# Expert numbers of quarters 1 to 7 of each pass, made from places by GpSimd instead of VectorE

## The chip, the cores and the metric

The kernel runs on one core of one Trainium2 chip. The metric is the device time of one execution in microseconds. Engines are named as the profile names them: PE is TensorE, DVE is VectorE, ACT is ScalarE, POOL is GpSimd, SP is the queue engine.

## The reference

Two layers of a transformer block over 256 latent tokens of width 1024 and 256 context tokens: three kinds of attention, a gated merge, and then an expert layer (PEER). What the change touches is how an expert is chosen:

```python
s = jnp.einsum('thpd,hpkd->thpk', q, keys)                 # 8 heads, two sides, 128 keys each
sv, si = lax.top_k(s, PEER_TOPK)                           # the 16 best keys of each side
cand_s = sv[:, :, 0, :, None] + sv[:, :, 1, None, :]       # 16 x 16 sums
cand_i = si[:, :, 0, :, None] * PEER_KEYS + si[:, :, 1, None, :]
top_s, pos = lax.top_k(cand_s, PEER_TOPK)                  # the 16 best sums and their places
e = jnp.take_along_axis(cand_i, pos, axis=-1)              # the expert numbers
g = jax.nn.softmax(top_s, axis=-1)
act = jax.nn.gelu(jnp.einsum('thkd,td->thk', u[e], tc))
return jnp.einsum('thk,thkd->td', g * act, v[e])
```

So each token picks 8 heads x 16 = 128 rows out of 16384, and of each row the part u is multiplied with the token and the part v is added up.

## The kernel before

**Passes.** The expert layer runs three times, in passes of 256 tokens: pass 0 (layer 0, latent tokens), pass 1 (layer 0, context tokens) and pass 2 (layer 1, latent tokens). A pass takes 256 *picks*. One pick is one gather: 128 partitions each fetch one expert row of 8 KB (u and v together), 1 MB, by an indirect DMA whose addresses are one column of `index`. An even pick serves 64 tokens, with two rows for each, and the odd one behind it the next 64. The 256 picks are divided into eight *quarters* of 32 (the name is the kernel's), each of which needs its own columns of `index` before its first gather.

**The loop over picks** stands on four engines, each in its own order:
- POOL (`gather`, L1848 to L1860) waits until the pair of picks that used the buffer eight picks ago is released (`row_used`), then issues the gather into one of eight buffers (L1854).
- DVE (`gather`, L2420 to L2432) waits for the rows (`rows_in`) and makes the dot of u with the token (L2426), 1024 elements.
- ACT makes the gelu, the weight and a scaled selection matrix of it (L1651, L1653, L1658).
- PE multiplies that matrix with v (L1252), four products for a pick, and releases a pair of buffers (`row_used`).

**What else runs there.** Between two dots DVE, ACT and PE each take steps of other work, called *ticks*: `PICKS_AT` says after which picks a tick of choosing experts stands, `TOKENS_AT` after which a tick of the rest (in pass 0 the whole attention and merge of the context tokens, in pass 1 the modulation and the projection of layer 1). Weight transfers for it come over SP's queue on the same sixteen DMA engines. The first quarter of a pass is chosen before its gathers, or for pass 1 at the end of pass 0.

**Choosing a quarter** (`picks_of`, DVE) takes seven ticks. Ticks 0 to 2 find the 16 best sums out of 112 candidates. Tick 3 turns their positions into *places*, for each pick a number 0 to 15 on either side (L2257 to L2269). Ticks 4 and 5 turn places into key numbers: for side w, compare the places with 0 to 15 (L2275, into `hot`, 128 x 512), multiply with the key numbers `sif` (L2276), add up over 16 (L2277, into `chosen`). Tick 5 then joins both sides to an expert number and writes `index` (L2280, L2283), tick 6 writes the softmax gates. `hot` lies in the same words as `work`, which the searches for the best use.

**Where the ticks stand.** Quarter 1 and quarter 2 of passes 0 and 2 have a tick every two picks, quarter 3 about every four, quarters 4 to 7 every four or five. In pass 1 all seven have one every two picks. Of quarter 2 of pass 2, for instance, tick 3 stands after the dot of pick 47 and tick 5 after that of pick 51; of its quarter 4 they stand after picks 97 and 107.

## Time and profile before

| | |
|---|---|
| median of 3 runs | 3107.65 us (3103.76 to 3109.70) |
| profiled execution | 3107.62 us, its span 3105.8 us |
| busy: PE, DVE, ACT, POOL | 2330.2 (75%), 1855.6 (60%), 1233.0 (40%), 849.2 (27%) us |
| mean granted PE clock | 0.866 |
| gathers (software queue): packets, MB, share of 16 DMA engines | 112032, 810.08, 63.8% |
| weights (hardware queue): packets, MB, share | 27216, 196.45, 16.4% |
| chain that ended last, by engine | PE 42%, DMA 30%, DVE 15%, ACT 6% |

The first gather of pass 0 starts 512.1 us into the span, that of pass 1 at 1321.5, that of pass 2 at 2426.8, and the last at 3071.1. The shares of busy time are averages over stages with different limits; what a change in the gather passes is worth has to be read there, from the share of the DMA engines in a window and from the times at which single gathers start and their dots start. A row's number in square brackets is idle time of its engine just before it, and behind the arrow what ended it.

### The profile page before, as it was taken

Reading aid. Unit: us, or ns where it says so; the run is one execution under the profiler, and the core shown is the slowest. Engines: PE = TensorE matmul, PEld = TensorE weight load, DVE = VectorE, ACT = ScalarE, POOL = GpSimd, SP = SyncE. Lnnn points to the kernel's source line nnn. Section 1 sums busy time; section 2 is a strip of 40 time slices with the busy share of each in tenths; the row PEclk is TensorE's granted clock in tenths of the full one; section 3 lists DMA queues with packets and bytes.
Section 4 is the critical chain, followed back from the end, with each engine's and each line's share of the span. In section 5 each row is a group of like instructions: output and inputs, shape, how many; then the busy total and the mean of one; then the engine's idle time right before and its main releaser. Section 6 shows DMA issues by size and latency. Waiting matters only on the chain.

```text
span 3105.8 us, 33307 instructions
## 1 busy us (share of the span) xinstructions
PE 2330.2 (75%) x11404; PEld 1352.9 (44%) x11404; DVE 1855.6 (60%) x4461; ACT 1233.0 (40%) x3361; POOL 849.2 (27%) x790
## 2 busy tenths in 40 slices
PE   5998998777669989665656688768998865555565
PEld 3787896443336645221212344217798621111111
DVE  3328655776855554586657554455864687666654
ACT  4215533344843243342333433244643434333333
POOL 0000001333332233343334443320000344444442
PEclk8999998988989999787767999969999988878777
DMA  6531246989989999999999999963044899999996
GB/s 255 217 133 48 96 162 244 413 347 378 394 345 389 402 421 407 383 401 421 388 421 405 414 421 421 421 288 122 22 163 150 332 383 422 421 421 421 419 422 288
DMA packets 139705, 1011.33 MB, mean 326 GB/s; under 512 B 15632, under 2 KB 15760, under 8 KB 17168
## 3 DMA queue, kind: packets, MB, share of 16 engines
q0 software_dynamic: 112032, 810.08, 63.8%
q1 hardware_dynamic: 27216, 196.45, 16.4%
q10 hardware_dynamic: 288, 2.69, 0.2%
q8 instruction: 90, 1.47, 0.2%
q14 instruction: 79, 0.65, 0.1%
HBM read 1008.10 MB, written 1.05 MB: 325 GB/s over the span
## 4 chain that ended last, share of the span: by engine, by line
PE 42%; DMA 30%; DVE 15%; ACT 6%; issue 3%; POOL 3%; ACTq 0%; POOLq 0%; DVEq 0%; SPq 0%
DMA att<-experts_in,att 28%; PE ps L1252 13%; DVE att L2426 5%; PE ps L612 4%; PE ps L1112 4%; PE ps L614 4%; PE ps L613 4%; POOL att L1854 3%; DMA ring<-stream_in 2%; PE ps L913 2%; DVE ring_lo L1900 2%; PE ps L1162 2%; ACT wt_hi L1356 2%; ACT att L1658 1%; PE ps L879 1%
## 5 line engine op out<-in xcount | busy, mean ns | idle before, releaser
L1252 PE MATMUL ps<-att 128*64 128x512 f32 x3072 | 977.8, 771 | 660.7 <-ACT att L1658 654.0
L1854 POOL DMA_INDIRECT att<-experts_in,att x768 | 838.9, 1092 | 1785.5 <-PE ps L1252 1202.0
L2426 DVE CUSTOM_DVE_ANT_0 att<-att 128x1024 f32<-128x1024 f32 x768 | 930.2, 1224 | 626.9 <-DMA att<-experts_in,att 615.4
L1252 PEld LDWEIGHTS ps<-att 128*64 128x64 f32 x3072 | 224.6, 163 | 1279.9 <-ACT att L1658 918.0
L1651 ACT ACTIVATE att<-att 128x1 f32<-128x1 f32 x768 | 154.4, 201 | 1050.2 <-DVE att L2426 1040.2
L1900 DVE TENSOR_TENSOR ring_lo<-ring,wt_hi 128x2048 fp32r<-128x2048 f32 x68 | 155.8, 2292 | 250.0 <-ACT wt_hi L1356 249.9
L1658 ACT ACTIVATE att<-const,att 128x64 f32<-128x64 f32 x768 | 267.1, 348 | 71.7 <-ACT att L1653 1.5
L1653 ACT ACTIVATE att<-att 128x1 f32<-128x1 f32 x768 | 226.1, 294 | 25.1
L1356 ACT ACTIVATE wt_hi<-ring 128x2048 fp32r<-128x2048 f32 x68 | 129.7, 1910 | 164.1 <-PE ps L614 86.8
L612 PE MATMUL ps<-h,wt_hi 128*128 128x256 f32 (+1 forms) x360 | 114.5, 318 | 19.7 <-DVE h L1914 11.0
L1844 POOL DMA_DIRECT2D att<-bias_in x16 | 8.9, 556 | 436.2 <-DVE stat L2093 413.1
L613 PE MATMUL ps<-h,wt_hi 128*128 128x256 f32 (+1 forms) x360 | 112.4, 312 | 0.0
L614 PE MATMUL ps<-h,ring_lo 128*128 128x256 f32 (+1 forms) x360 | 112.2, 312 | 0.0
L1175 PE MATMUL ps<-spare,ring 128*128 128x256 f32 x384 | 87.5, 383 | 0.0
L1112 PE MATMUL ps<-spare,ring 128*128 128x256 f32 x384 | 86.9, 379 | 0.0
L612 PEld LDWEIGHTS ps<-h,wt_hi 128*128 128x128 f32 x360 | 71.8, 199 | 29.8 <-DVE ring_lo L1900 14.3
L770 PE MATMUL ps<-att,ring 128*128 128x256 f32 x336 | 81.1, 396 | 0.0
L1175 PEld LDWEIGHTS ps<-spare,ring 128*128 128x128 f32 x384 | 71.5, 190 | 22.0 <-issue 13.0
L1112 PEld LDWEIGHTS ps<-spare,ring 128*128 128x128 f32 x384 | 72.9, 190 | 11.1 <-issue 1.3
L770 PEld LDWEIGHTS ps<-att,ring 128*128 128x128 f32 x336 | 64.3, 197 | 28.3 <-issue 19.9
L613 PEld LDWEIGHTS ps<-h,wt_hi 128*128 128x128 f32 x360 | 71.8, 199 | 2.7
L614 PEld LDWEIGHTS ps<-h,ring_lo 128*128 128x128 f32 x360 | 71.7, 199 | 2.9
(252 smaller groups left out, 3678.4 us busy)
## 6 DMA issues: line engine op xcount, KB each, us to landing
ring<-stream_in SPq DMA_DIRECT2D x183, 1024.0 KB
att<-experts_in,att POOLq DMA_INDIRECT x768
att<-bias_in POOLq DMA_DIRECT2D x16, 256.0 KB, 2.9
spare<-stream_in SPq DMA_DIRECT2D x3, 1024.0 KB, 7.0
x<-x_in ACTq DMA_DIRECT2D x1, 2048.0 KB, 8.2
out<-att SPq DMA_DIRECT2D x1, 1024.0 KB, 3.9
const<-const_in ACTq DMA_DIRECT2D x1, 576.0 KB, 4.3
att<-lambda_in SPq DMA_DIRECT2D x1, 256.0 KB, 11.4
```

Source lines behind the costliest of these rows:

```text
L612: mm(dst, a[0], b[0], start=start, stop=False)
L613: mm(dst, a[0], b[1], start=False, stop=False)
L614: return mm(dst, a[1], b[0], start=False, stop=stop)
L1112: last = mm(ps[:, 2 + item % 6, 0:N_CTX], raw_slot(p0, b), src, start=(c == 0), stop=(c == count - 1))
L1175: last = mm(ps[:, pq_bank(r, u), 0:N_LAT], raw_slot(p0, u * DC + c), h2_plain[:, c, :], start=(c == 0), stop=(c == DC - 1))
L1252: last = mm(ps[HALF * s:HALF * (s + 1), d, :], diag[:, (m + s) % DIAGS, :], rows[:, (m + s) % SLOTS, D + 512 * d:D + 512 * (d + 1)], start ...
L1356: nc.scalar.activation(wt_hi[:, d % 2, :], ring[:, DENSE[d] % RING, :], ACT.Copy)\
L1653: nc.scalar.activation(acts[:, n:n + 1], acts[:, n:n + 1], ACT.Copy, scale=gates[:, r % 2, n:n + 1])\
L1658: nc.scalar.activation(diag[:, m % DIAGS, :], fold, ACT.Copy, scale=acts[:, n:n + 1])\
L1854: nc.gpsimd.indirect_dma_start(out=rows[:, m % SLOTS, :], out_offset=None, in_=experts_in, in_offset=bass.IndirectOffsetOnAxis(ap=index[:, ...
L1900: v.tensor_tensor(ring_lo[:, DENSE[d] % RING, :], ring[:, DENSE[d] % RING, :], wt_hi[:, d % 2, :], ALU.subtract)\
L2426: v.tensor_tensor_reduce(out=u_row, in0=u_row, in1=dup[:, n // HK, n % 2, :], scale=1.0, scalar=0.0, op0=ALU.mult, op1=ALU.add, accum_out= ...
```

## The change

POOL makes `chosen` from the places for quarters 1 to 7 of each pass; quarter 0 stays on DVE. The table `chosen_before` says ahead of which gathers the two sides stand: side 0 nine gathers behind the pick of tick 3, side 1 two gathers later. For quarter 2 of pass 2 these are gathers 56 and 58, for quarter 4 gathers 106 and 108, for quarter 6 of pass 1 gathers 108 and 110. POOL subtracts, compares with zero, multiplies, and adds up by halving: seven instructions for a side, each waiting for the one before by a semaphore. DVE's tick 4 is empty, and tick 5 waits for both sides.

```diff
@@
+def chosen_before(r):
+    at = {}
+    tick = SIDE_TICKS if r != 1 else 1 + SIDE_TICKS
+    for q in range(1, QUARTERS):
+        slot = PICKS_AT[r][tick + PICK_PLACES] | 1
+        for w in range(2):
+            at[min(slot + SLOTS + 1, q * QUARTER - 2) + 2 * w] = q, w
+        tick += PICK_TICKS
+        if q == 1:
+            tick += len(CTX_SIDES) * SIDE_TICKS + (1 if r == 1 else 0)
+    return at
@@ gpsimd
+            def after_step(ins):
+                steps_done[0] += 1
+                ins.then_inc(pool_order, 1)
+                pool.wait_ge(pool_order, steps_done[0])
+
+            def chosen_of(r, q, w):
+                pair = [P, 2, TOPK, TOPK]
+                steps16 = iota[:, 0:TOPK].unsqueeze(1).unsqueeze(1).to_broadcast(pair)
+                pool.wait_ge(places_ready, (QUARTERS - 1) * r + q)
+                at = places[:, w * QUARTER:(w + 1) * QUARTER].rearrange("p (h k) -> p h k", h=2)
+                after_step(nc.gpsimd.tensor_tensor(hot, steps16, at.unsqueeze(3).to_broadcast(pair), ALU.subtract))
+                after_step(nc.gpsimd.tensor_scalar(hot, hot, 0.0, None, ALU.is_equal))
+                after_step(nc.gpsimd.tensor_tensor(hot, hot, sif[:, :, w, :].unsqueeze(2).to_broadcast(pair), ALU.mult))
+                for half in (8, 4, 2):
+                    after_step(nc.gpsimd.tensor_tensor(hot[:, :, :, 0:half], hot[:, :, :, 0:half],
+                                                       hot[:, :, :, half:2 * half], ALU.add))
+                nc.gpsimd.tensor_tensor(chosen[:, w, :].rearrange("p (h k) -> p h k", h=2).unsqueeze(3),
+                                        hot[:, :, :, 0:1], hot[:, :, :, 1:2], ALU.add).then_inc(chosen_ready, 1)
+                pool.wait_ge(chosen_ready, 2 * ((QUARTERS - 1) * r + q - 1) + w + 1)
+
             def gather(r):
+                before = chosen_before(r)
                 for n in range(PICKS):
                     m = r * PICKS + n
+                    if n in before:
+                        chosen_of(r, *before[n])
@@ picks_of on DVE
+                if q:
+                    v.tensor_tensor(places[:, QUARTER:2 * QUARTER], next2, low2, ALU.add).then_inc(places_ready, 1)
+                    yield
+                    yield
+                    dve.wait_ge(chosen_ready, 2 * ((QUARTERS - 1) * r + q))
+                else:
+                    link(v.tensor_tensor(places[:, QUARTER:2 * QUARTER], next2, low2, ALU.add))
+                    yield
+                    for w in range(2):
+                        chosen_at_first(w)      # the three instructions as before
+                        if w == 0:
+                            yield
```

POOL, pass 2 from its start, as before (`att` is the large tile in which buffers, index and scratch lie):

```order
L1844 DMA att<-bias_in 128x512
L1844 DMA att<-bias_in 128x512 [waits max_ready] x6
L1854 DMA att<-experts_in,att 128x2048 [waits row_used,index_ready]
L1854 DMA att<-experts_in,att 128x2048 [waits row_used] x31
L1854 DMA att<-experts_in,att 128x2048 [waits row_used,index_ready]
```

POOL, pass 2 around gathers 106 to 108, as changed:

```order
L1899 DMA att<-experts_in,att 128x2048 [waits row_used] x9
L1879 TENSOR_TENSOR att<-const,att 128x512 [waits places_ready]
L1880 TENSOR_SCALAR att<-att 128x512 [waits pool_order]
L1881 TENSOR_TENSOR att<-att 128x512 [waits pool_order]
L1883 TENSOR_TENSOR att<-att 128x32x8 [waits pool_order]
L1883 TENSOR_TENSOR att<-att 128x32x4 [waits pool_order]
L1883 TENSOR_TENSOR att<-att 128x32x2 [waits pool_order]
L1885 TENSOR_TENSOR att<-att 128x32 [waits pool_order]
L1899 DMA att<-experts_in,att 128x2048 [waits row_used,chosen_ready]
L1899 DMA att<-experts_in,att 128x2048 [waits row_used]
L1879 TENSOR_TENSOR att<-const,att 128x512 [waits places_ready]
```

Seven instructions now stand ahead of gather 106 and seven ahead of gather 108, where only gathers stood.

DVE, quarter 2 of pass 2, from tick 4 to the dot behind tick 5, as before (L2426 is the dot, `rows_in` the semaphore of its buffer):

```order
L2275 TENSOR_TENSOR att<-const,att 128x512
L2276 TENSOR_TENSOR att<-att 128x512 [waits dve_order]
L2277 TENSOR_REDUCE att<-att 128x32 [waits dve_order]
L2426 ISA att<-att 128x1024 [waits rows_in2,dve_order]
L2426 ISA att 128x1
L2426 ISA att<-att 128x1024 [waits rows_in3]
L2426 ISA att 128x1
L2275 TENSOR_TENSOR att<-const,att 128x512
L2276 TENSOR_TENSOR att<-att 128x512 [waits dve_order]
L2277 TENSOR_REDUCE att<-att 128x32 [waits dve_order]
L2280 SCALAR_TENSOR_TENSOR att<-att 128x32 [waits dve_order]
L2283 TENSOR_SCALAR att<-att 64x16 [waits dve_order]
```

DVE at the same place, as changed (L2480 is the dot, L2334 and L2337 are what L2280 and L2283 were):

```order
L2480 ISA att 128x1
L2480 ISA att<-att 128x1024 [waits rows_in2]
L2480 ISA att 128x1
L2480 ISA att<-att 128x1024 [waits rows_in3]
L2480 ISA att 128x1
L2334 SCALAR_TENSOR_TENSOR att<-att 128x32 [waits chosen_ready]
L2337 TENSOR_SCALAR att<-att 64x16 [waits dve_order]
L2337 TENSOR_SCALAR att<-att 64x16 x3
L2480 ISA att<-att 128x1024 [waits rows_in4]
```

The six instructions are gone, and the first instruction of the index waits for POOL, with the dot of pick 52 behind it.

## Rows read from the trace of the kernel before

**Rows 1.** The page, busy share of the DMA engines in 40 slices of 77.6 us:

```profile
DMA  6531246989989999999999999963044899999996
```

**Rows 2.** Windows: stretch, us, busy PE, PEld, DVE, ACT, POOL (count), PEclk, DMA share, GB/s:

```profile
600.00:660.00 60.00, 37.22 (x125) 14.59 (x126) 55.11 (x214) 25.84 (x79) 19.09 (x18) 0.76 0.86 338
740.00:880.00 140.00, 94.64 (x528) 44.42 (x528) 115.05 (x275) 105.35 (x289) 49.94 (x48) 0.87 0.92 361
...
1500.00:1520.00 20.00, 12.84 (x55) 4.06 (x56) 12.73 (x29) 11.29 (x35) 8.20 (x8) 0.76 0.76 292
...
2560.00:3060.00 500.00, 281.77 (x806) 62.98 (x802) 307.31 (x664) 185.86 (x617) 219.24 (x201) 0.78 1.01 421
```

**Rows 3.** Timeline, pass 1: gather 60 (POOL) and its dot (DVE); start, length, idle before:

```profile
1506.85 0.94 POOL L1854 DMA_INDIRECT att<-experts_in,att  x1 [10.89 <-PE ps L1252]
...
1512.67 1.23 DVE L2426 CUSTOM_DVE_ANT_0 att<-att 128x1024 f32<-128x1024 f32 x1 [1.96 <-DMA att<-experts_in,att]
```

**Rows 4.** Timeline, pass 2, quarter 4: gathers 105, 106, 108 and the dot of 107:

```profile
2693.03 1.26 POOL L1854 DMA_INDIRECT att<-experts_in,att  x1 [0.30 <-issue]
...
2698.31 0.94 POOL L1854 DMA_INDIRECT att<-experts_in,att  x1 [4.02 <-PE ps L1252]
...
2701.73 0.94 POOL L1854 DMA_INDIRECT att<-experts_in,att  x1 [1.23 <-PE ps L1252]
...
2712.14 1.23 DVE L2426 CUSTOM_DVE_ANT_0 att<-att 128x1024 f32<-128x1024 f32 x1 [1.25 <-DMA att<-experts_in,att]
```

**Rows 5.** Groups by form (count, busy us, mean ns, idle before), and all gathers (ns min/median/max):

```profile
L2276 DVE TENSOR_TENSOR att<-att 128x512 f32<-128x512 f32 x48 | 33.2, 692 | 1.7
L2275 DVE TENSOR_TENSOR att<-const,att 128x512 f32<-128x512 f32 x48 | 33.0, 688 | 0.2
L2277 DVE TENSOR_REDUCE att<-att 128x32 f32<-128x512 f32 x48 | 32.9, 686 | 1.6
...
L2181 DVE TENSOR_TENSOR att<-att 128x256 f32<-128x256 f32 x32 | 13.6, 425 | 1.1
...
L1854 POOL DMA_INDIRECT att<-experts_in,att x768: 932/937/1992, 512.1 to 3071.1; - x192
```

**Rows 6.** Timeline, pass 2, quarter 2: gathers 55, 60; dots 51, 53, 57; index:

```profile
2568.96 1.03 POOL L1854 DMA_INDIRECT att<-experts_in,att  x1 [0.30 <-issue]
...
2571.59 1.22 DVE L2426 CUSTOM_DVE_ANT_0 att<-att 128x1024 f32<-128x1024 f32 x1 [0.43 <-DMA att<-experts_in,att]
...
2575.13 0.72 DVE L2283 TENSOR_SCALAR att<-att 64x16 uint32<-64x16 f32 x4
...
2577.03 1.22 DVE L2426 CUSTOM_DVE_ANT_0 att<-att 128x1024 f32<-128x1024 f32 x1
...
2582.92 1.09 POOL L1854 DMA_INDIRECT att<-experts_in,att  x1 [3.76 <-PE ps L1252]
...
2587.04 1.22 DVE L2426 CUSTOM_DVE_ANT_0 att<-att 128x1024 f32<-128x1024 f32 x1 [1.24 <-DMA att<-experts_in,att]
```

**Rows 7.** Timeline, pass 1, quarter 6: gathers 104 and 107, dot of 107:

```profile
1649.75 0.94 POOL L1854 DMA_INDIRECT att<-experts_in,att  x1 [10.36 <-PE ps L1252]
...
1654.54 1.03 POOL L1854 DMA_INDIRECT att<-experts_in,att  x1 [0.30 <-issue]
...
1664.52 1.22 DVE L2426 CUSTOM_DVE_ANT_0 att<-att 128x1024 f32<-128x1024 f32 x1 [1.02 <-DMA att<-experts_in,att]
```

**Rows 8.** Timeline, DVE's search behind quarter 1, passes 0 and 2, waiting for PE:

```profile
597.07 0.90 DVE L2202 MAX8 att<-ps 128x8 f32<-128x128 f32 x4 [5.63 <-PE ps L998]
...
2504.53 0.89 DVE L2202 MAX8 att<-ps 128x8 f32<-128x128 f32 x4 [5.76 <-PE ps L998]
```

**Rows 9.** Timeline, pass 1: gather 80 and its dot:

```profile
1566.95 1.68 POOL L1854 DMA_INDIRECT att<-experts_in,att  x1 [7.56 <-PE ps L1252]
...
1584.11 1.23 DVE L2426 CUSTOM_DVE_ANT_0 att<-att 128x1024 f32<-128x1024 f32 x1 [1.84 <-DMA att<-experts_in,att]
```

More of the change, by code:

```diff
@@ L82 @@
             BIASED[STEP0[_l] + _n] = len(BIASED)
-PICK_TICKS, PICK_EXP = 7, 4
+PICK_TICKS, PICK_EXP, PICK_PLACES = 7, 4, 3
 SIDE_TICKS = 2
@@ L128 @@
              spread(1, (REST_UNIT_TICKS, 28)) + spread(HK + 4, (UPDATE_TICKS, 16))]
+def chosen_before(r):
[8 more added lines that the diff above has]
+            tick += len(CTX_SIDES) * SIDE_TICKS + (1 if r == 1 else 0)
+    assert tick == len(PICKS_AT[r])
+    return at
 def due(at, n):
@@ L405, in build @@
         mod_cols_copied = sem("mod_cols_copied")
+        places_ready = sem("places_ready")
+        chosen_ready = sem("chosen_ready")
+        pool_order = sem("pool_order")
         mod_ready = sem("mod_ready")
@@ L1845, in biases @@
                         .then_inc(bias_arrived[b % 2], 16)
+            steps_done = [0]
+            def after_step(ins):
[16 more added lines that the diff above has]
+                pool.wait_ge(chosen_ready, 2 * ((QUARTERS - 1) * r + q - 1) + w + 1)
             def gather(r):
+                before = chosen_before(r)
                 for n in range(PICKS):
                     m = r * PICKS + n
+                    if n in before:
+                        chosen_of(r, *before[n])
                     if n % QUARTER == 0:
@@ L2224, in sides_of, with chosen_at_first @@
                 yield
+            def chosen_at_first(w):
+                pair = [P, 2, TOPK, TOPK]
+                steps16 = iota[:, 0:TOPK].unsqueeze(1).unsqueeze(1).to_broadcast(pair)
+                at = places[:, w * QUARTER:(w + 1) * QUARTER].rearrange("p (h k) -> p h k", h=2)
+                link(v.tensor_tensor(hot, steps16, at.unsqueeze(3).to_broadcast(pair), ALU.is_equal))
+                link(v.tensor_tensor(hot, hot, sif[:, :, w, :].unsqueeze(2).to_broadcast(pair), ALU.mult))
+                link(v.tensor_reduce(chosen[:, w, :].rearrange("p (h k) -> p h k", h=2), hot, AX.X, ALU.add))
             def picks_of(r, l, q):
@@ L2235, in placed @@
                         .rearrange("p (k s) -> p s k", s=2)[:, s, :]
-                pair = [P, 2, TOPK, TOPK]
                 dve.wait_ge(sides_found, 8 * r + 4 * tt + g + 1)
@@ L2268, in picks_of @@
                 link(v.scalar_tensor_tensor(next2, by16, 4.0, next2, ALU.is_lt, ALU.mult))
-                link(v.tensor_tensor(places[:, QUARTER:2 * QUARTER], next2, low2, ALU.add))
-                yield
-                steps16 = iota[:, 0:TOPK].unsqueeze(1).unsqueeze(1).to_broadcast(pair)
-                for w in range(2):
-                    at = places[:, w * QUARTER:(w + 1) * QUARTER].rearrange("p (h k) -> p h k", h=2)
-                    link(v.tensor_tensor(hot, steps16, at.unsqueeze(3).to_broadcast(pair), ALU.is_equal))
-                    link(v.tensor_tensor(hot, hot, sif[:, :, w, :].unsqueeze(2).to_broadcast(pair), ALU.mult))
-                    link(v.tensor_reduce(chosen[:, w, :].rearrange("p (h k) -> p h k", h=2), hot, AX.X, ALU.add))
-                    if w == 0:
-                        yield
+                if q:
[10 more added lines that the diff above has]
+                            yield
                 link(v.scalar_tensor_tensor(partsf[:, 0:QUARTER], chosen[:, 0, :], float(KEYS), chosen[:, 1, :],
```

## The prediction

> **What bounds the kernel now.** Read the row of slices first [rows 1]: the sixteen DMA engines stand at eight or nine tenths from slice 8 to slice 26 and again from slice 32 to slice 39, which is where the three gather passes lie. Then the windows [rows 2]: over the last 500 us of pass 2 the DMA share is 1.01 at 421 GB/s while DVE is busy 307 us of 500 and POOL 219. One gather moves 1 MB, 2.49 us at that rate. DVE is nearly full only in short stretches (55 of 60 us at 600 to 660, 115 of 140 at 740 to 880), and there the DMA share falls to 0.86 and 0.92. So time is gained only where DMA runs dry for DVE's sake, and lost wherever a gather is issued too late. This is why the two questions are how much DVE relief falls into the dry stretches, and how late GpSimd gets.
>
> **How late may it be?** The shortest way from issue to use in the trace is 5.8 us: the gather at 1506.85 came after GpSimd had waited 10.89 us, DMA had run dry (share 0.76 in 1500 to 1520, [rows 2]), and its dot began at 1512.67 [rows 3]. In the saturated part of pass 2 the way is longer because others are queued ahead: gather 106 of the pass goes out at 2698.31 and gather 107's dot starts at 2712.14 [rows 4]. A gather costs nothing as long as its issue plus 5.8 us is not behind the landing of the one before plus 2.49.
>
> **What is removed.** Per quarter DVE loses six instructions, twice 0.69 + 0.69 + 0.69 = 2.07 us [rows 5], 4.1 us, in 21 of 24 quarters: 87 us of 1856. In the saturated stretches DVE's idle time grows by that and nothing else happens. Quarters 3 and 4 of pass 0 lie in 740 to 880, where DVE is short: at most 2 x 4.1 = 8 us. I take half, since what follows in that stretch is not DVE's alone (ACT is busy 105 of the 140 us, [rows 2]): **minus 4 us**.
>
> **What is added.** Two chains of seven GpSimd instructions per quarter, each waiting for the one before: subtract, compare and multiply on 512 elements, then additions on 256, 128, 64 and 32. The trace has no GpSimd arithmetic, so the chain's price D is bounded. From below: DVE's prices, three times 0.69 and four times the 0.42 of a 256-element addition [rows 5], 3.8 us. From above: seven times GpSimd's own step, 0.94 us plus the 0.30 us in front of it [rows 4, 5], 8.7 us. I take seven times 0.94, **D = 6.6 us**, since a GpSimd row is nearer to GpSimd than DVE's, and since the wait for its own semaphore must cost something over 3.8.
>
> The Trainium skill (GPSIMD Engine Reference, section 3.1) measures a two-input addition at 1.96 times DVE's time. By that page alone the chain would be an estimated 6 to 7 us, and the sum nearly the one below.
>
> **Where the chains stand.** Chain 0 comes ahead of the gather nine behind the pick at which DVE writes the places, chain 1 two gathers on. Queued behind each are the gathers. DVE no longer computes; two ticks behind the places it waits for both chains, and behind that wait stand its dots, without which ACT and TensorE release no row. Where ticks are two picks apart (quarters 1 and 2 of passes 0 and 2, all of pass 1: the *tight* ones) the wait comes after four dots, while chain 1 needs the release of the second of them. Where they are four or five apart (the *spread* ones) DVE finds the numbers ready.
>
> **A spread quarter,** pass 2, quarter 4 [rows 4]. Gather 105 ends at 2694.3. Chain 0 runs to 2700.9, most of it in the 4.02 us that GpSimd waited anyway; 106 and 107 go out by 2703.1; chain 1 ends at 2709.7. Gather 108 goes out then instead of at 2701.73 and lands at 2715.5 at best. Row 107's dot is at 2712.1, so 2714.6 was due: 0.9 us lost. At D = 8.7 it is 5.1, at 3.8 nothing. Exposed like this are quarters 3 to 7 of pass 2 and, DMA being near full, 6 and 7 of pass 0: 7 x 0.9 = **6 us**. Quarter 5 of pass 0 lies under work that holds TensorE full.
>
> **A tight quarter,** pass 2, quarter 2 [rows 6]. Chain 0 from 2570.0 to 2576.6, gathers 56 and 57 until 2578.8, chain 1 until 2585.4. Gather 58 lands at 2591.2 at best, due 2587.0 + 2.5: 1.7 us. DVE stands from the end of dot 51 (2572.8) until 2585.4; the index takes 1.0 (0.72 of it its four last instructions), dot 52 1.2, so dot 53 starts at 2587.6 instead of 2577.03. From that dot to gather 60, which needs its release, were 2582.92 - 2577.03 = 5.9 us. So gather 60 goes out at 2593.5, lands at 2599.3, due 2596.2: 3.1 us more. Together 4.8; at D = 8.7 it is 9.0, at 3.8 nothing. Exposed are quarter 2 of each pass and quarter 7 of pass 1: 4 x 4.8 = **19 us**. Quarters 1, 3, 4 and 5 of pass 1 have weight transfers beside the gathers and a longer way: gather 80 of pass 1 took 17 us from 1566.95 to its dot at 1584.11 [rows 9]. I put them at nothing.
>
> Quarter 6 of pass 1 is worse [rows 7]. GpSimd has just waited 10.36 us for TensorE, the DMA queue is short, and the chains come right behind gather 107 (1654.54, end 1655.6; its dot at 1664.52). Chain 0 to 1662.2, gather 108 lands 1668.0 instead of 1667.0; chain 1 from 1664.4 to 1671.0, gather 110 lands 1676.8, 3.8 late; DVE freed at 1671.0, dot 105 at 1673.2, gather 112 at 1679.1, landing 3.1 late: **8 us**.
>
> Quarter 1 of passes 0 and 2 stops DVE for 8 and 12 us by the same reckoning, right ahead of the stretch in which DVE is full. Behind it DVE waited 5.6 and 5.8 us for key products [rows 8], which takes some of it back: 2 and 6, **8 us**.
>
> **The sum.** 6 + 19 + 8 + 8 - 4 = 37 us. The profiled execution took 3107.62 us (span 3105.8), the median of the runs is 3107.65, so nothing has to be converted: **3145 us**. With D = 3.8: nothing in the first two terms, 2 in quarter 6, 2 in the first quarters, minus 8 relief, 3104. With D = 8.7: 36 + 36 + 12 + 16 - 4 = 96, 3204.
>
> **Rivals.**
> 1. *The chains are cheap* (D below 5). Every delay fits into the queue, the relief is small: about 3104. For it: GpSimd idles over half the time in pass 2. Against it: the wait for its own semaphore behind each of seven instructions.
> 2. *The two engines get in each other's way.* A gather takes 932 to 1992 ns with a median of 937 [rows 5]; what lengthens the long ones no row says, and DVE's instructions beside them are the nearest candidate. If the 2.7 dots (1.22 us each) that fall into a chain hold it for half their time, D is 6.6 + 1.6 = 8.2 and the sum, between the two ends, 82 us: 3190. The Trainium skill (SBUF — State Buffer, Summary: rules for kernel authors) says that a DVE instruction with two SBUF inputs and a GpSimd instruction that reads SBUF block each other fully. No row here shows it: GpSimd reads no tile for arithmetic before.
> 3. *Faster: DVE is what empties the queue.* The first quarter of each pass feeds the stretches where DVE is full, and quarters 3 and 4 of pass 0 lie in one. If all five give back their 4.1 us and the chains are hidden, 21 us come off: 3087. It decides the matter if D stays under 4 and DVE never stands at its wait. Against it: at 2560 to 3060 DMA is full whatever DVE does.
> 4. *The change does less than it says.* Not so by the order of instructions: 42 chains stand on GpSimd, and one extra set-up instruction ahead of the first.
>
> **Chances.** Forecast (about 3120 to 3170) 0.45; rival 2 or a dear chain 0.23; rival 1 0.17, most of it within 0.2%; rival 3 0.14. About 0.2% is what a measurement of this kernel can tell from no change, 6 us. Faster 0.16, same 0.14, slower 0.70. The range leaves out rival 3 and the far end of a dear chain: 3098 to 3206.
>
> **What would show it.** GpSimd's seven instructions from first start to last end: D. A DVE wait for GpSimd at the first index operation, 8 to 13 us in tight quarters and none in spread ones. DMA share below 1.01 in windows around the second and seventh quarters, and still 1.01 where only spread quarters lie if D is under 6. In 740 to 880 a share over 0.92. I am wrong if D is under 5, if DMA stays at 1.01 through tight quarters, or if a dot lasts longer than 1.22 us beside a chain.

## The result and the profile after

The changed kernel takes 3206.59 us (median of four runs, 3203.95 to 3211.24), the kernel before beside it on the same chip 3108.62 us. The ratio is 1.0326, with an interval of 1.0313 to 1.0339. The change makes the kernel 98 us slower; the forecast was 3145 us in a range of 3098 to 3206. The sign was right; the forecast cost of 37 us is less than half of the measured one.

The profiled execution took 3204.31 us, its span 3202.5. It is compared with the one before (3107.62), so 96.7 us are to be found. First the page: busy share of the DMA engines in 40 slices, and below it the chain that ended last, by engine.

```profile
DMA  6631347989889999999998999942154999999997
...
PE 40%; DMA 24%; DVE 15%; POOL 11%; ACT 6%; issue 4%; ACTq 0%; POOLq 0%; DVEq 0%; SPq 0%
```

The slices look full as in [rows 1], which is why they are not enough. In the chain that ended last POOL now has 11% (3% on the page of before), and DMA 24% instead of 30%. The windows that answer to two of [rows 2] (stretch, us, busy PE, PEld, DVE, ACT, POOL with counts, granted PE clock, DMA share, GB/s) say it more clearly:

```profile
740.00:880.00 140.00, 93.86 (x505) 42.48 (x501) 112.72 (x258) 104.14 (x281) 77.17 (x74) 0.83 0.91 361
2560.00:3060.00 500.00, 264.23 (x768) 62.13 (x768) 294.08 (x764) 172.25 (x569) 285.81 (x265) 0.74 0.93 376
```

In 2560 to 3060 the share of the DMA engines fell from 1.01 to 0.93 and the rate from 421 to 376 GB/s, although DVE has less to do than before. Pass 2 starts 43 us later in this trace, so the window holds somewhat earlier picks; moved by 43 us, to 2603 to 3103, it gives 0.94 and 383 GB/s, the same picture. In 740 to 880, where relief was expected, it is 0.91 where it was 0.92: nothing was gained.

The chains by form (line, engine, operation, shapes, count, busy us, mean ns, idle before), with the dot behind them as the last line:

```profile
L1880 POOL TENSOR_SCALAR att<-att 128x512 f32<-128x512 f32 x42 | 72.3, 1721 | 3.7
L1881 POOL TENSOR_TENSOR att<-att 128x512 f32<-128x512 f32 x42 | 59.5, 1417 | 3.5
L1879 POOL TENSOR_TENSOR att<-const,att 128x512 f32<-128x512 f32 x42 | 46.7, 1112 | 0.9
L1883 POOL TENSOR_TENSOR att<-att 128x256 f32<-128x256 f32 x42 | 41.7, 994 | 3.3
L1883 POOL TENSOR_TENSOR att<-att 128x128 f32<-128x128 f32 x42 | 23.3, 555 | 3.3
L1885 POOL TENSOR_TENSOR att<-att 128x32 f32<-128x32 f32 x42 | 18.3, 435 | 3.3
L1883 POOL TENSOR_TENSOR att<-att 128x64 f32<-128x64 f32 x42 | 15.0, 357 | 3.3
...
L2480 DVE CUSTOM_DVE_ANT_0 att<-att 128x1024 f32<-128x1024 f32 x768 | 947.5, 1248 | 645.8 <-DMA att<-experts_in,att 642.8
```

The busy times add up to 6.6 us for a chain, and with the small gaps between its instructions the mean length of the 42 chains, first start to last end, is 7.1 us. Thirteen of them take 6.0 us, all in tight quarters, where DVE stands at its wait; the longest takes 9.2.

Where the 96.7 us lie is read from the timeline, from each pass's first gather to its last dot, and within a pass from how much later than before the dot of a given pick comes:

| place | forecast | measured |
|---|---|---|
| pass 2, quarters 3 to 7 (spread) | 4.5 | 36.0 |
| pass 2, quarters 1 and 2 (tight) | 6 + 4.8 | 16.3 |
| pass 1, quarters 6 and 7 | 8 + 4.8 | 15.9 |
| pass 1, quarters 1 to 5 | 4.8 | 10.7 |
| pass 0, all, relief included | 2 + 4.8 + 1.8 - 4 | 16.0 |
| outside the passes | 0 | 1.8 |
| sum | 37.5 | 96.7 |

The small rows are rough, since the table compares two single executions: in traces whose chains leave a pass alone, that pass still differs from before by up to 5 us (pass 1 of e5_apart2 4.7 longer, pass 0 of e7_tight2 3.8 shorter). Over half of what is missing is in the first line, which is beyond that. Here is its quarter 4 as it ran: the gathers 105 to 108, both chains, and of DVE the dots that matter (start, length, engine, operation, idle time before and what ended it).

```profile
2760.69 0.94 POOL L1899 DMA_INDIRECT att<-experts_in,att  x1 [0.30 <-issue]
...
2761.64 1.33 POOL L1879 TENSOR_TENSOR att<-const,att 128x512 f32<-128x512 f32 x1
...
2768.58 1.10 POOL L1885 TENSOR_TENSOR att<-att 128x32 f32<-128x32 f32 x1
...
2769.96 1.01 POOL L1899 DMA_INDIRECT att<-experts_in,att  x1 [0.28 <-POOL att L1885]
...
2771.28 1.54 POOL L1899 DMA_INDIRECT att<-experts_in,att  x1 [0.31 <-issue]
...
2772.85 1.06 POOL L1879 TENSOR_TENSOR att<-const,att 128x512 f32<-128x512 f32 x1
2773.23 1.77 DVE L2480 CUSTOM_DVE_ANT_0 att<-att 128x1024 f32<-128x1024 f32 x1 [1.23 <-DMA att<-experts_in,att]
...
2774.00 2.37 POOL L1880 TENSOR_SCALAR att<-att 128x512 f32<-128x512 f32 x1
...
2775.72 1.23 DVE L2480 CUSTOM_DVE_ANT_0 att<-att 128x1024 f32<-128x1024 f32 x1 [0.71 <-DMA att<-experts_in,att]
...
2779.75 1.23 DVE L2480 CUSTOM_DVE_ANT_0 att<-att 128x1024 f32<-128x1024 f32 x1 [2.79 <-DMA att<-experts_in,att]
...
2781.35 1.01 POOL L1899 DMA_INDIRECT att<-experts_in,att  x1 [0.28 <-POOL att L1885]
...
2787.04 1.23 DVE L2480 CUSTOM_DVE_ANT_0 att<-att 128x1024 f32<-128x1024 f32 x1 [4.71 <-DMA att<-experts_in,att]
```

Chain 0 lasts 8.04 us and chain 1 8.2. Gather 106 goes out at 2769.96, while the rows of 105 are still on their way (its dot is the one at 2773.23). The dot of 106 starts 5.76 us after its issue, at 2775.72, 2.49 us behind that of 105: chain 0 has used up the backlog to the last, but costs nothing yet. From there on it does cost: the dots of 107 and 108 follow at 4.0 and 7.3 us instead of 2.49, and that of 109, shown at the end of this document, at 3.0. Together that is 6.9 us. No dot here waits for POOL, as forecast; those behind the chains wait for their rows.

The same lines show the two engines in each other's way. The dot at 2773.23 takes 1.77 us instead of 1.22 while a subtract runs, and the compare behind it takes 2.37 us instead of the 1.50 of undisturbed chains. The Trainium skill (SBUF — State Buffer, Summary: rules for kernel authors) has a DVE instruction with two SBUF inputs and a GpSimd instruction that reads SBUF block each other fully. By that rule the trace agrees roughly: subtract and dot overlapped from 2773.23 to 2773.91, 0.68 us, and the dot grew by 0.55; dot and compare overlapped for 1.0 us, and the compare grew by 0.87. (The record of the compare also overlaps the dot at 2775.72, by 0.65 us, and that dot did not grow, so the ends of these records are not exact.) The longest dot beside a chain in this trace takes 2.33 us.

### The profile page after: what moved, and what is told of

Its sections match the earlier page's. It is cut to its first block, busy times and chain, and to the rows that moved or that the text cites. A ratio compares the mean times of both kernels' runs of the same rounds, so it can differ in the third digit from the quotient of the medians.

```text
span 3202.5 us, 33480 instructions
## 1 busy us (share of the span) xinstructions
PE 2337.3 (73%) x11404; PEld 1357.9 (42%) x11404; DVE 1796.7 (56%) x4335; ACT 1233.9 (39%) x3361; POOL 1137.5 (36%) x1084
## 3 DMA queue, kind: packets, MB, share of 16 engines
q1 hardware_dynamic: 27216, 196.45, 15.9%
## 4 chain that ended last, share of the span: by engine, by line
PE 40%; DMA 24%; DVE 15%; POOL 11%; ACT 6%; issue 4%; ACTq 0%; POOLq 0%; DVEq 0%; SPq 0%
DMA att<-experts_in,att 22%; PE ps L1270 12%; DVE att L2480 6%; POOL att L1899 5%; PE ps L630 4%; PE ps L631 4%; PE ps L632 4%; PE ps L1130 4%; POOL att L1880 2%; PE ps L931 2%; POOL att L1883 2%; DVE ring_lo L1945 1%; ACT wt_hi L1374 1%; PE ps L1031 1%; ACT att L1676 1%
## 5 line engine op out<-in xcount | busy, mean ns | idle before, releaser
L1899 POOL DMA_INDIRECT att<-experts_in,att x768 | 850.3, 1107 | 1571.1 <-PE ps L1270 965.4
L2480 DVE CUSTOM_DVE_ANT_0 att<-att 128x1024 f32<-128x1024 f32 x768 | 947.5, 1248 | 645.8 <-DMA att<-experts_in,att 642.8
L2334 DVE SCALAR_TENSOR_TENSOR att<-att 128x32 f32<-128x32 f32 x24 | 4.6, 191 | 144.7 <-POOL att L1885 144.4
L1883 POOL TENSOR_TENSOR att<-att 128x256 f32<-128x256 f32 (+2 forms) x126 | 80.0, 635 | 9.9
L630 PEld LDWEIGHTS ps<-h,wt_hi 128*128 128x128 f32 x360 | 70.5, 196 | 26.2 <-DVE ring_lo L1945 12.8
```

Of the source, the lines that this page charges most:

```text
L630: mm(dst, a[0], b[0], start=start, stop=False)
L1899: nc.gpsimd.indirect_dma_start(out=rows[:, m % SLOTS, :], out_offset=None, in_=experts_in, in_offset=bass.IndirectOffsetOnAxis(ap=index[:, ...
L2480: v.tensor_tensor_reduce(out=u_row, in0=u_row, in1=dup[:, n // HK, n % 2, :], scale=1.0, scalar=0.0, op0=ALU.mult, op1=ALU.add, accum_out= ...
```

## The experiments

**The theories,** with the letters that the recorded expectations use. A: late gathers are what costs in the spread quarters. It leaves two questions, whether the chains are longer than thought, because they run beside dots (the expectations say "the port"), and whether the queue holds less than thought, so that a spread quarter starts to lose at a shorter chain. B: the delay of one quarter is handed on to the next. C: DVE's wait for POOL is what costs, not the late gathers. A last question is whether the six instructions per quarter that DVE lost give back the 4 us of the forecast. The runs below vary which quarters go through POOL, how long the chains are, whether they read anything, and whether DVE waits. Edits are shown against the changed kernel. Times of before are medians of the runs made on the same chip in the same comparison.

### Only the spread quarters of pass 2, and only the tight ones

```diff
+ON = [(2, 3), (2, 4), (2, 5), (2, 6), (2, 7)]      # e2_spread2;  e7_tight2: [(2, 1), (2, 2)]
@@ chosen_before
+        if (r, q) in ON:
             for w in range(2):
@@ picks_of on DVE
-                if q:
+                if (r, q) in ON:
```

Quarters that are not listed stay on DVE, as in the kernel before.

> Only quarters 3 to 7 of pass 2 are made by GpSimd, exactly as in the change; all others stay on DVE. In the changed kernel these five quarters made pass 2 6 to 9 us longer each (36 us in sum). Theory A, late gathers (the chains keep GpSimd from issuing, the DMA queue runs dry): about 36 us, 3145. Theory B, the delay is handed on from the tight quarters ahead of them: under 10 us, below 3120.

> Only quarters 1 and 2 of pass 2 are made by GpSimd as in the change. In the changed kernel pass 2 lost 11.4 us at quarter 1 and 5.8 at quarter 2. If the terms add up: 17 us, 3125. If the pass as a whole decides: another sum, since 17 and 36 us would not give the 52 of the changed kernel.

Measured: spread quarters alone 3146.73 us against 3111.13, ratio 1.0116 (1.0099 to 1.0133), +35.6 us; tight ones alone 3130.64, ratio 1.0068 (1.0051 to 1.0085), +19.5. In the traces pass 2 grew by 35.7 and by 18.3 us, together 54 where the changed kernel has 52.3. So the parts add up in this pass, nothing is handed on from one quarter to the next (B fails), and the spread quarters' 7.1 us each, where the forecast had 0.9, stand by themselves.

### The same instructions without their purpose, and writes alone

e3_beside2 lets POOL run the seven instructions on constants into memory of its own, while DVE makes its own numbers and waits for nothing. e4_write2 has seven memsets in their place, e11, e15 and e12 other sizes and numbers of them. All five touch quarters 3 to 7 of pass 2 only, and what POOL makes is not used.

```diff
@@ e3_beside2, chosen_of
-                pool.wait_ge(places_ready, (QUARTERS - 1) * r + q)
-                at = places[:, w * QUARTER:(w + 1) * QUARTER].rearrange("p (h k) -> p h k", h=2)
+                own = words(FREE + 4096, 512).rearrange("p (h k i) -> p h k i", h=2, k=TOPK)
+                at = iota[:, 0:QUARTER].rearrange("p (h k) -> p h k", h=2)
...
@@ e4_write2, chosen_of (e11: [1215] * 7, e15: [1110] * 5, e12: [1000] * 4)
+                for count in [1000] * 7:
+                    after_step(nc.gpsimd.memset(words(FREE + 4096, count), 0.0))
@@ all five, picks_of on DVE
-                if q:
+                if False:
```

> Quarters 3 to 7 of pass 2: DVE computes its own numbers and waits for nothing, as before; GpSimd runs the same fourteen instructions ahead of the same gathers on constants and on memory of its own, and nobody uses their result. Theory A, late gathers: as long as with the real chains, within 3 us (3140 to 3148). Theory C, DVE's wait at the index matters here too: nearly as before, under 3115.

> As the run beside it, but each chain is seven memsets of 1000 elements, which read nothing from SBUF; I estimate 6 to 7 us for a chain from the 1.06 us that GpSimd's first instruction on 512 elements takes. Theory A with the shared port (chains of 6.0 us alone become 7 to 9 us beside dots): the seven memsets all take the same time, dots stay at 1.22 us, and the quarters cost less than the real chains at equal busy time, about 1 us each at 6 us. Theory A without the port (length alone decides): the cost at a chain of 6 to 7 us is that of the real chains, 7 us each.

> Quarters 3 to 7 of pass 2 with chains of seven memsets of 1215 elements, 8.3 us instead of 6.9, reading nothing and used by nobody, DVE as before. If a chain's length is all that counts (the port acts by making the real chain longer and in no other way): as the read-and-write chains of the same length, 36 to 40 us, 3147 to 3151. If the real chains also cost through slower dots: clearly less, under 3142.

> Quarters 3 to 7 of pass 2 alone, and in place of each chain four memsets of 1000 words (0.93 us each), each waiting for the one before, into memory that nobody reads; DVE makes its own numbers. With seven memsets, a chain of 6.88 us, the pass grew by 24.8 us; at 8.13 us by 31.5. Here a chain should last 3.9 us. The forecast's slack says that a chain of 3.8 us is hidden: nothing, 3108 to 3111 us. If the loss goes on in a straight line through the two measured ones (5.4 us more for 2.5 us more of GpSimd per quarter at most), then about 1.9 us per quarter remain: 3116 to 3120. In between means a threshold that lies lower than the forecast put it, at about 5 us.

> As the other memset kernels, quarters 3 to 7 of pass 2 alone, with five memsets of 1110 words per chain, about 5.4 us. Measured so far: nothing lost at 3.9 us, 25 us at 6.9, 31.5 at 8.1 (by the pass in the trace). The forecast's slack hides every chain up to 6.1 us: 3107 to 3109. A straight line from nothing at 3.9 to 25 at 6.9 gives 12: 3117 to 3122. If so the slack is about 4 us, and the error lies in how long a chain may be, more than in how long it is.

Measured, with the loss per quarter as a fifth of the difference of medians:

| kernel | chain, us | median and before | ratio | per quarter |
|---|---|---|---|---|
| e12_write2_short | 3.92 | 3107.61, 3107.32 | 0.9998 (0.9986 to 1.0010) | 0.1 |
| e15_write2_mid | 5.36 | 3116.09, 3109.32 | 1.0016 (1.0003 to 1.0029) | 1.4 |
| e4_write2 | 6.88 | 3135.98, 3111.13 | 1.0081 (1.0064 to 1.0098) | 5.0 |
| e11_write2_long | 8.13 | 3146.57, 3108.62 | 1.0132 (1.0099 to 1.0165) | 7.6 |
| e2_spread2, real | 6.9 to 9.2, mean 8.07 | 3146.73, 3111.13 | 1.0116 (1.0099 to 1.0133) | 7.1 |
| e3_beside2 | 7.9 to 9.0, mean 8.43 | 3147.63, 3111.13 | 1.0114 (1.0097 to 1.0131) | 7.3 |

The forecast's own reckoning of a spread quarter is a straight line, twice the chain's excess over 6.15 us: 0.9 at 6.6 and 5.1 at 8.7. The four memset kernels lie on a line of the same slope with another foot, twice the excess over about 4.4 us: 0, 1.9, 5.0 and 7.5. The real chain's 8.07 us gives 7.3 on it, and 7.1 were measured. So the slope was right, and two things were wrong, the foot of the line and the chain's length. The fit is not sharp at its upper end: the four runs of e11_write2_long lie between 3137 and 3156 us, and in its trace the pass grew by 31.5 us, 6.3 per quarter, where it grew by 35.7 in that of e2_spread2 and by 40.0 in that of e3_beside2. So it is not excluded that reading costs about a microsecond per quarter beyond the longer chain. e4_write2 was expected to cost about 1 us per quarter or 7, and cost 5.0: so a chain of that length costs much by itself, but not all. e15_write2_mid cost less than the line through 3.9 and 6.9 us that was expected to hold (12 us), and more than the forecast (nothing). e3_beside2 agrees with theory A: it does the same without any wait of DVE and costs what the real ones cost, so in spread quarters C has no visible part. Windows of the same 400 us (columns as above) for chains of 3.9, 6.9 and 8.1 us:

```profile
2600.00:3000.00 400.00, 236.45 (x648) 51.94 (x644) 250.18 (x549) 150.21 (x497) 221.07 (x199) 0.72 1.01 419
```
```profile
2600.00:3000.00 400.00, 221.34 (x612) 48.92 (x610) 238.08 (x528) 141.53 (x467) 231.14 (x221) 0.75 0.96 392
```
```profile
2600.00:3000.00 400.00, 216.90 (x600) 48.21 (x596) 237.33 (x523) 138.77 (x458) 231.83 (x217) 0.74 0.94 385
```

At 3.9 us the DMA share stays at 1.01, as in the kernel before, and the chains are free.

The memsets also settle what lengthens a chain. In the trace of e4_write2 from 2600 to 3050, which holds quarters 3 to 7, the second row below is all memsets of all chains and the first the dots of the same stretch, and under them the dots of e2_spread2:

```profile
L2479 DVE CUSTOM_DVE_ANT_0 att<-att 128x1024 f32<-128x1024 f32 x170 | 208.4, 1227 | 185.2 <-DMA att<-experts_in,att 184.5
...
L1886 POOL MEMSET att<- 128x1000 f32 x70 | 65.3, 933 | 3.5
```
```profile
L2490 DVE CUSTOM_DVE_ANT_0 att<-att 128x1024 f32<-128x1024 f32 x165 | 208.2, 1263 | 199.7 <-DMA att<-experts_in,att 199.0 <-DVE att L2260 0.4
```

Each of the memset chains that the trace has whole takes 6.87 to 6.89 us wherever it lies, and the dots beside it keep their mean of 1227 ns, that of the kernel before in this stretch. Beside chains that read, the dots' mean is 1263 ns and the chains take 6.9 to 9.2 us where they take 6.0 when DVE stands. So reading is what makes the two engines collide, about 2 us per chain: near the size that the forecast's second rival gave it (1.6 us). The section of the Trainium skill cited above sets the same bound, a GpSimd instruction that reads SBUF; the trace agrees here too, with memset chains of 6.88 us and dots of 1227 ns.

Why the foot is at 4.4 us can be read in e4_write2, whose chains are nearly as long as the forecast's 6.6. POOL in quarter 4 of pass 2, and the dots of 107 and 108:

```profile
2697.24 0.94 POOL L1898 DMA_INDIRECT att<-experts_in,att  x1 [0.30 <-issue]
2698.18 6.88 POOL L1886 MEMSET att<- 128x1000 f32 x7
2705.32 1.56 POOL L1898 DMA_INDIRECT att<-experts_in,att  x1 [0.27 <-POOL att L1886]
2707.19 1.03 POOL L1898 DMA_INDIRECT att<-experts_in,att  x1 [0.30 <-issue]
2708.22 6.88 POOL L1886 MEMSET att<- 128x1000 f32 x7
2715.37 1.66 POOL L1898 DMA_INDIRECT att<-experts_in,att  x1 [0.27 <-POOL att L1886]
```
```profile
2714.99 1.23 DVE L2479 CUSTOM_DVE_ANT_0 att<-att 128x1024 f32<-128x1024 f32 x1 [1.51 <-DMA att<-experts_in,att]
...
2721.84 1.23 DVE L2479 CUSTOM_DVE_ANT_0 att<-att 128x1024 f32<-128x1024 f32 x1 [2.59 <-DMA att<-experts_in,att]
...
2724.72 1.23 DVE L2479 CUSTOM_DVE_ANT_0 att<-att 128x1024 f32<-128x1024 f32 x1 [1.65 <-DMA att<-experts_in,att]
```

The quarter loses 4.4 us at dot 108 (6.85 behind dot 107, not 2.49) and 0.4 at dot 109, 4.8 in all. The forecast's way would give 1.5 for a chain of 6.88 us. Four small errors, here all on one side, make the 3.3 us between:
- dot 107 came 16.8 us after chain 0 began, and 17.8 were assumed: 1.0. The queue's backlog at that point depends on which gathers have just gone out.
- from the start of chain 0 to gather 108 POOL needed 3.4 us beside the two chains, and 2.2 were assumed: 1.2. The two gathers between took 1.56 and 1.03 us and not 0.94, and a step stands ahead of each.
- gather 108 took 6.5 us to its dot, and 5.8, the shortest way in the trace of before, was assumed: 0.7.
- gather 109 landed 2.88 behind it and not 2.49: 0.4.

Quarter 4 of the changed kernel, shown above, gives 1.2, 1.2, -0.1 and 0.6 for the same four: there gather 108 took 5.69 us to its dot. So three of the four come back beside real chains, and the third belongs to this run. With the forecast's own formula for chains of 8.05 and 8.22 us, 4.0, they add up to the 6.9 us that the quarter lost.

### The second chain further back, and the chains in pieces

```diff
@@ e5_apart2, chosen_before
-            at[min(slot + SLOTS + 1, q * QUARTER - 2) + 2 * w] = q, w
+            at[min(slot + SLOTS + 1, q * QUARTER - 6) + 6 * w] = q, w
@@ e6_pieces2, chosen_before
+            for k in range(6):
+                at[slot + SLOTS + 1 + 2 * k] = q, k // 3, k % 3
```

Both serve quarters 3 to 7 of pass 2 only. In e6_pieces2 a chain stands in three pieces (subtract and compare; multiply and first addition; the rest) ahead of every second gather, and DVE makes the index one tick later.

> Quarters 3 to 7 of pass 2 on GpSimd with the same instructions, but the second chain stands six gathers behind the first instead of two, so that GpSimd can catch up in between. Theory A (the DMA queue is drained by two chains in a row, since one chain of 8 us alone fits into the 11.6 us between its start and the landing of the last gather issued): the 36 us fall below 12, under 3123. If the mere sum of GpSimd's work decides, or the port's effect on the dots, they stay at 30 or more.

> The same five quarters, the fourteen instructions in six pieces of 1 to 3 us, each ahead of every second gather, and DVE's index moved one tick later so that it does not wait. GpSimd does the same work beside the same dots. Theory A: each piece fits into the 1 to 4 us that GpSimd waits between pairs; within 5 us of the kernel before. If the shared port matters by itself: still over 3120.

Measured: e5_apart2 3128.79 us against 3108.62, ratio 1.0067 (1.0048 to 1.0085), +20 us, more than the 12 us that were expected at most, and less than the 30 that the other theories asked for. In its trace pass 2 grew by 10.6 us, pass 1, which has no chains in it, by 4.7, and the rest lies outside the passes, so that pass 2's own share is less certain than the median's. The run also changes a second thing: the later chain makes DVE wait at the index of every one of the five quarters, 9.4, 4.75 and three times 3.2 us. The second of these waits:

```profile
2730.78 0.19 DVE L2344 SCALAR_TENSOR_TENSOR att<-att 128x32 f32<-128x32 f32 x1 [4.75 <-POOL att L1895]
```

How much of the cost is the first chain (7.9 to 9.2 us here, the second 6.0 to 6.9) and how much DVE's wait is not separated, so this run only shows that moving the chains apart helps, not that one chain by itself is too long. e6_pieces2 3113.76 (ten runs), ratio 1.0019 (1.0005 to 1.0032), +5 us for work that in one piece costs 35.6. Its pieces take 1.1 to 3.5 us, and behind each a pair of gathers goes out. DVE did wait here too, against what was expected, 6.65 us in the first of the five quarters and 3.3 in the others. That the cost goes with the longest stretch without a gather, and not with POOL's work, is shown by e6_pieces2 beside e2_spread2: POOL has the same fourteen instructions per quarter in both.

### The relief

```diff
@@ e8_relief: quarters 1 to 7 of all passes, DVE
-                    dve.wait_ge(chosen_ready, 2 * ((QUARTERS - 1) * r + q))
@@ gather on POOL
-                    if n in before:
-                        chosen_of(r, *before[n])
```

DVE leaves its six instructions out and nobody makes the numbers: the index is formed from old ones. The gathers then fetch other rows, and in 2560 to 3060 they still run at 421 GB/s.

> DVE leaves the six instructions out in quarters 1 to 7 of every pass and nobody makes the numbers (the expert numbers of those quarters come from the first quarter's places, so part of the computation is left out). This is DVE's relief alone, the most that the change could gain. The forecast said 4 us, its rival 21. DMA is full in most of the passes, so I expect 3 to 10 us under the kernel before, 3100 to 3107.

Measured: 3105.38 us against 3108.62, ratio 0.9982 (0.9968 to 0.9996). The 87 us that DVE no longer computes are worth 3 us by medians, 6 by the ratio, and its interval goes from 1 to 10. Where they are gained isn't shown: the profiled execution took 3110.14 us, and in it no pass is shorter than before by more than 1.2 us; in 740 to 880 DVE is busy 103 us and not 115, and the DMA share is 0.92 as before. With the steps where they stand now this is about the most that the change can bring.

```diff
@@ e14_pass0_mid
+ON = [(0, 3), (0, 4)]
```

> Only quarters 3 and 4 of pass 0 on GpSimd as in the change, the two in which DVE is nearly full and where the forecast counted a gain of 4 us. The forecast: 3104 to 3105 us. The trace of the changed kernel showed 2 to 3 us of loss there: 3110 to 3112 if the chains take back what the relief gives.

Measured: 3114.82 us against 3107.32 (twelve runs), ratio 1.0021 (1.0009 to 1.0033), +7.5 us where the forecast had -4 and 3 to 5 were expected. The window 820 to 860, with the two chains of quarter 4, in the kernel before and in this one:

```profile
820.00:860.00 40.00, 29.01 (x158) 12.92 (x155) 33.04 (x73) 32.15 (x86) 14.86 (x15) 0.87 0.99 393
```
```profile
820.00:860.00 40.00, 26.38 (x140) 11.60 (x136) 32.51 (x66) 28.40 (x75) 31.02 (x28) 0.87 0.74 286
```

DVE is as busy as before, and the DMA share falls from 0.99 to 0.74: here too the queue runs dry behind the chains (8.0 and 8.9 us). In this trace pass 0 grew by 10.1 us, nearly all of it at quarter 4; the execution took 3124.51 us, 10 more than the median, so the size is that of the median. In the trace of the changed kernel the same two quarters grew by 3.3 us only; why is not known. The forecast read this stretch as short of DVE's time alone and gave the gathers slack that they don't have.

### The tight quarters: stop or late gathers

The chains of e3_beside2, on quarters 1 and 2 of pass 2 (e10_tight_beside2), and quarters 6 and 7 of pass 1 with real chains (e13_pass1_end) and with those beside (e16_pass1_beside):

```diff
+ON = [(2, 1), (2, 2)]      # e10_tight_beside2;  e13_pass1_end and e16_pass1_beside: [(1, 6), (1, 7)]
```

> Quarters 1 and 2 of pass 2 alone: the same seven GpSimd instructions per chain, on constants and into memory of their own, with the gathers queued behind them as in the change; DVE makes its own numbers and waits for nothing. With the real wait the two quarters cost 18.3 us of the pass (13.9 and 5.2 in the first and second). By the forecast's split the late gathers alone make 1.7 of the second quarter's 4.8, and DVE's stop the rest: 3111 to 3116 us if so. If the late gathers are the whole of it, 3124 to 3130, as with the real wait.

> Only quarters 6 and 7 of pass 1 on GpSimd as in the change, all others on DVE. The forecast: 8 + 4.8, 3121 us. The trace of the changed kernel: 18 us between pick 103 and pick 119 and nothing in quarter 7, 3125 to 3128, if what it shows there belongs to these quarters and isn't handed on from the five quarters before.

> Quarters 6 and 7 of pass 1 alone, chains on constants and into memory of their own, DVE makes its own numbers and waits for nothing. With the real wait these two quarters cost 18 us by medians and the pass 20 in the trace, and DVE stood 20.8 us at quarter 6, since the four gathers ahead of the first chain had themselves waited 13.6 us for TensorE. If DVE's stop is the cause, at most half of it is left: 3108 to 3114. If late gathers are, 3120 or more.

| kernel | median and before | ratio | in its trace, by quarter |
|---|---|---|---|
| e7_tight2, DVE waits | 3130.64, 3111.13 | 1.0068 (1.0051 to 1.0085) | 13.9, then 5.2 |
| e10_tight_beside2 | 3120.11, 3107.32 | 1.0044 (1.0028 to 1.0060) | 4.5, then 8.2 |
| e13_pass1_end, DVE waits | 3125.32, 3107.32 | 1.0047 (1.0028 to 1.0067) | 12.9, then 7.6 |
| e16_pass1_beside | 3123.80, 3109.32 | 1.0050 (1.0035 to 1.0065) | 9.5, then 7.3 |

In pass 1 the cut between the quarters is the dot of pick 117, the last ahead of DVE's second wait. The profiled execution of e13_pass1_end took 3138.07 us, 13 more than the median, of which 20.5 lie in these two quarters.

C fails as a general answer: without any stop of DVE two thirds of the cost remain in pass 2 (12.8 of 19.5 us) and four fifths in pass 1 (14.5 of 18). e10_tight_beside2 came out between the two times that were expected for it (3111 to 3116 and 3124 to 3130). The reading by quarters is finer. Where DVE stops, the gathers behind catch up with it: behind the stop in e13_pass1_end gathers 104 to 107 are used 20 to 22 us after their issue, and the 18.3 us by which the dot of 104 is late shrink to 11.5 by that of 111. Without the stop 108 and 110 are used 6.6 and 6.3 us after theirs: here the late gathers cost by themselves. Quarter 7 costs 7.6 us with a stop of 12 us and 7.3 without one, quarter 2 of pass 2 5.2 with and 8.2 without. So a stop and late gathers are not added up; that the larger of the two counts fits these numbers, but is not shown by them. The second stop of e13_pass1_end:

```profile
1720.63 0.19 DVE L2344 SCALAR_TENSOR_TENSOR att<-att 128x32 f32<-128x32 f32 x1 [11.97 <-POOL att L1895]
```

Not a clean comparison in one point: with DVE at work the chains are longer (6.9 to 9.8 us) than with DVE at a stand (6.0 to 7.1).

In the first quarter of pass 2 the stop does decide (13.9 against 4.5). Two rows of e7_tight2, DVE's wait in the quarter and the wait that follows in the searches behind it:

```profile
2498.92 0.19 DVE L2344 SCALAR_TENSOR_TENSOR att<-att 128x32 f32<-128x32 f32 x1 [17.00 <-POOL att L1895]
...
2519.25 0.89 DVE L2257 MAX8 att<-ps 128x8 f32<-128x128 f32 x4 [5.77 <-PE ps L1026]
```

DVE stood for 17.0 us. The wait for key products, which was to take half of it back, is as long as it was in [rows 8], 5.77 against 5.76: PE makes those products behind the gather products, which come from DVE's own dots. It was no slack.

## Why the prediction was wrong, point by point

- **What bounds the kernel**: right. DMA was the limit, and a gather issued too late is what costs. In the windows taken of spread quarters (2560 to 3060 of pass 2, 820 to 860 of pass 0) the loss is lost DMA share.
- **D = 6.6 us**: the undisturbed chain takes 6.0 and the 42 have a mean of 7.1, inside the bounds of 3.8 and 8.7; the longest, 9.2, is outside. That seven times GpSimd's gather step came near the sum is luck: undisturbed the seven instructions take from 1.50 down to 0.24 us. By the Trainium skill (GPSIMD Engine Reference, section 3.1) the estimate was 6 to 7 us; the undisturbed chain agrees. But the mean hides the case that counts: beside dots, which is where all spread chains run, it takes 8.0 in pass 2 of the changed kernel and 8.1 in e2_spread2.
- **The spread quarter, 0.9 us**: this is the step that failed, with 36 us for 4.5 in pass 2. Its mechanism and its slope held. It was mis-sized by two terms. The foot of the line was put at 6.15 us, from a backlog of a single instance, the shortest way of 5.8 us and gathers of 0.94 us, while the memset kernels put it near 4.4; that is 3.5 us per quarter. The chain beside dots is 1.5 us longer than assumed; that is 2.9 us per quarter. 0.9 + 3.5 + 2.9 is 7.3, and 7.1 were measured. The foot rests on the fit of four kernels; quarter 4 of the changed kernel alone would put it at 4.7.
- **That DVE finds the numbers ready in spread quarters**: right but for 4.75 us in the third quarter of pass 2 and 0.49 in the last.
- **The tight quarters**: of quarter 2 of pass 2 (forecast 4.8, trace of after 5.8, alone 5.2) the size was right and the way to it was not, since its two parts don't add. Quarter 6 of pass 1 (forecast 8) cost 8.4 us in the changed kernel and 12.9 alone in e13_pass1_end, quarter 7 (forecast 4.8) 7.6 in both. DVE stopped ahead of dot 104, as reckoned. How long it stands there depends on the four gathers ahead of the first chain, which PE held for 10.4 us in the kernel before, 9.3 in the changed one and 13.9 in e13_pass1_end; the stop was 16.9 and 20.8 us. The row is that of the changed kernel:

```profile
1696.08 0.19 DVE L2334 SCALAR_TENSOR_TENSOR att<-att 128x32 f32<-128x32 f32 x1 [16.92 <-POOL att L1885]
```

- **Quarter 1 of pass 2, 6 us**: 10.9 in the trace of after. The step that failed is the one that let a later wait for PE give half of the stop back.
- **Relief, minus 4**: failed in sign where it was placed (+7.5 in e14_pass0_mid, with its chains). Without chains there is one over the whole kernel, 3 to 6 us with an interval of 1 to 10, but its trace does not show it in this stretch.
- **The rivals**: the second was nearest to what happened, 3190 with a chain of 8.2 us. The first, that chains under 5 us are free, is true at 3.9 us; between that and 5.4, where the loss has begun, nothing was run. The third, 21 us of gain, has its bound in e8_relief. The price of the collision, 1.6 us of chain, was worked out in the second, but kept out of the sum because no row of before showed GpSimd reading for arithmetic.
- **The range**: its upper end missed the median by less than a microsecond. It stood for a dear chain only (the sum with D = 8.7 is 3204), and held nothing for an error of the slack. That this sum comes so near is luck: no such chain was there on the mean, and for chains of 8.1 us the forecast's formula gives 3.9 us per spread quarter and not 7.1.
- **The signs named ahead**: a dot longer than 1.22 us beside a chain was named as one that proves the forecast wrong, and it appeared (1.42 and 1.77 in quarter 4, 2.33 at most). DVE's waits in tight quarters were 8.2 to 16.9 us, not 8 to 13. The chances given to the four outcomes add up to 0.99.

What stays open: the granted PE clock of 2560 to 3060 is 0.74 where it was 0.78, in e12_write2_short (0.72 in 2600 to 3000) even without any loss of time; whether it costs anything elsewhere was not tried. The 10.7 us of quarters 1 to 5 of pass 1 and some 8 of pass 0 were not taken apart.

## What to carry to other kernels

An engine that issues the transfers of a saturated queue has a longest absence, not a share of idle time: GpSimd was busy 27% of the span, and a chain was free at 3.9 us, cost 1.4 us at 5.4 and somewhat over two more for each further microsecond, for two chains, in the fully loaded last pass. Cut such work into pieces shorter than what the queue holds, with transfers between them: the same instructions then cost 5 us instead of 36. And when a slack is the difference of two long paths, don't take it from the best instance of each: a few errors of 0.4 to 1.2 us, nearly all on one side, were worth more here than the whole term.

## What the hardware showed that was not expected

- A one-input compare with a constant on 128x512 takes GpSimd 1.50 us undisturbed, more than the two-input subtract (1.06) or multiply (1.26) on the same shape. A 32-element addition takes 0.24 undisturbed, and 1.10 to 1.31 where it starts while a dot runs.
- Collisions with DVE depend on whether GpSimd reads: 933 ns for a memset of 1000 words wherever it stands, and dots at 1227 ns beside it.
- The first gather into an empty queue is used 5.6 to 6.5 us after its issue, and the second, though issued 1.3 to 2 us behind it, 2.5 to 4.7 us after the first, mostly 3 to 4, and not 2.49: in quarter 4 of the changed kernel

```profile
2790.09 1.23 DVE L2480 CUSTOM_DVE_ANT_0 att<-att 128x1024 f32<-128x1024 f32 x1 [1.81 <-DMA att<-experts_in,att]
```

  is the dot of gather 109, 3.04 us behind that of 108.
